# Last two expert items of a layer taken together: both down projections behind both up projections, in a two-layer trunk with routed experts

## The reference, cut to what matters

```
def hybrid_layer(x, norm1, w_in, a_ln_g, a_ln_b, a_ws, a_bs, ret_gn, w_out, norm2,
                 router_g, router_gb, router_e, router_eb, w_gate, w_up, w_down):
    bsz, seq, _ = x.shape
    h = rms_norm(x, norm1)
    z = h @ w_in
...
    x = x + jnp.concatenate([a_out, b_out, c_out], axis=-1) @ w_out
    x = x + hier_moe(rms_norm(x, norm2), router_g, router_gb, router_e, router_eb,
                     w_gate, w_up, w_down)
    return x
...
def hier_moe(h, router_g, router_gb, router_e, router_eb, w_gate, w_up, w_down):
...
    combine = jnp.sum(jax.nn.one_hot(expert_id, N_EXPERTS, dtype=jnp.float32)
                      * top_w[..., None], axis=1)
    y = jnp.zeros((n_tok, d), jnp.float32)
    for e in range(N_EXPERTS):
        he = jax.nn.silu(t @ w_gate[e]) * (t @ w_up[e])
        y = y + combine[:, e:e + 1] * (he @ w_down[e]).astype(jnp.float32)
    return y.astype(h.dtype).reshape(bsz, seq, d)
```

## Time and profile before

| | |
|---|---|
| median of 3 runs | 716.33 us (715.28 to 717.75) |
| the profiled execution | 716.53 us, of which its span is 714.6 us |
| TensorE (PE) busy | 670.8 us, 94% of the span |
| VectorE (DVE) busy | 308.9 us, 43% |
| ScalarE (ACT) busy | 191.9 us, 27% |
| read from HBM | 239.32 MB |
| granted TensorE clock | full until the last slice |

### The profile page before, as it was taken

One profiled execution on the slowest core, in us unless ns is written; L12 is line 12 of the kernel. 1 busy time (PEld: TensorE's weight loads), 2 busy tenths in 40 slices (PEclk: granted clock), 3 DMA queues, 4 the chain that ended last, 5 costly groups with the idle time before them and its releaser, 6 DMA issues.

```text
span 714.6 us, 9124 instructions
## 1 busy us (share of the span) xinstructions
PE 670.8 (94%) x3452; PEld 384.6 (54%) x3452; DVE 308.9 (43%) x605; ACT 191.9 (27%) x342; POOL 16.3 (2%) x29
## 2 busy tenths in 40 slices
PE   6998999999999999998999989999999999999984
PEld 5877778733543543542388768785353453453431
DVE  3479886711331321321474798865131331231224
ACT  3438434311201201201154445442111111111102
POOL 3000000200000000000020000000000000000000
PEclk9999999999999999999999999999999999999998
DMA  9974039999999999999986330898999999999991
GB/s 334 341 276 168 1 137 389 372 421 404 422 406 394 422 421 421 421 421 421 402 285 223 130 118 30 328 389 338 424 403 423 403 423 415 421 422 419 421 414 63
DMA packets 46026, 240.95 MB, mean 337 GB/s; under 512 B 3457, under 2 KB 3649, under 8 KB 21281
## 3 DMA queue, kind: packets, MB, share of 16 engines
q1 hardware_dynamic: 44800, 238.21, 82.8%
q0 software_dynamic: 1040, 2.04, 1.1%
q10 hardware_dynamic: 144, 0.13, 0.1%
HBM read 239.32 MB, written 1.05 MB: 336 GB/s over the span
## 4 chain that ended last, share of the span: by engine, by line
PE 74%; DMA 10%; DVE 8%; ACT 4%; issue 2%; SPq 1%; DVEq 0%; PEldq 0%; ACTq 0%
PE psum L1059 28%; PE psum L746 14%; PE psum L1091 14%; DMA up_w<-in_w_up 7%; PE psum L1043 4%; DMA down_w<-in_w_in 3%; PE psum L1004 3%; PE psum L766 2%; ACT xT L671 1%; PE psum L973 1%; DVE scores L1200 1%; PE psum L1071 1%; PE psum L914 1%; PE psum L731 1%; DVE scores L1182 1%
## 5 line engine op out<-in xcount | busy, mean ns | idle before, releaser
L746 PE MATMUL psum<-piece_hi,hT_part 128*128 128x512 f32 x416 | 130.2, 394 | 3.4 <-ACT gate_b L611 1.5
L1059 PE MATMUL psum<-up_w,xT 128*64 128x512 f32 x512 | 113.3, 594 | 4.9 <-DMA up_w<-in_w_up 4.9
L1091 PE MATMUL psum<-down_w,scores 128*64 128x512 f32 x512 | 113.5, 595 | 0.6 <-ACT scores L680 0.6
L746 PEld LDWEIGHTS psum<-piece_hi,hT_part 128*128 128x128 f32 x416 | 76.7, 188 | 21.0 <-issue 5.8
L746 PE MATMUL psum<-piece_lo,hT_part 128*128 128x512 f32 x208 | 81.2, 391 | 0.0
L1059 PEld LDWEIGHTS psum<-up_w,xT 128*64 128x64 f32 x512 | 37.7, 137 | 76.7 <-issue 68.2
L1091 PEld LDWEIGHTS psum<-down_w,scores 128*64 128x64 f32 x512 | 36.6, 137 | 64.7 <-issue 63.1
L1495 DVE TENSOR_TENSOR y_lo<-psum,y_hi 128x512 fp32r<-128x512 f32 x32 | 22.1, 691 | 110.9 <-ACT y_hi L687 110.9
L1059 PE MATMUL psum<-gate_a,xT 128*64 128x512 f32 x256 | 56.6, 593 | 1.2 <-DMA gate_a<-in_w_gate 1.2
L1059 PE MATMUL psum<-gate_b,xT 128*64 128x512 f32 x256 | 56.4, 593 | 0.0
L1474 DVE SCALAR_TENSOR_TENSOR work<-work,psum 128x512 f32<-128x512 f32 x16 | 11.0, 687 | 100.8 <-ACT work L678 100.8
(11 more groups left out here) (234 smaller groups left out, 763.2 us busy)
## 6 DMA issues: line engine op xcount, KB each, us to landing
up_w<-in_w_up SPq DMA_DIRECT2D x32, 2048.0 KB, 13.7
down_w<-in_w_down SPq DMA_DIRECT2D x64, 1024.0 KB, 11.7
gate_b<-in_w_gate SPq DMA_DIRECT2D x32, 1024.0 KB, 13.0
gate_a<-in_w_gate SPq DMA_DIRECT2D x32, 1024.0 KB, 15.9
up_w<-in_w_in SPq DMA_DIRECT2D x6, 2048.0 KB, 13.4
down_w<-in_w_in SPq DMA_DIRECT2D x4, 2048.0 KB, 21.3
down_w<-in_w_out SPq DMA_DIRECT2D x4, 2048.0 KB, 7.8
up_w<-in_w_in SPq DMA_DIRECT2D x4, 1024.0 KB, 8.4
```

The source lines that it names most:

```text
L746: ins = pe.matmul(o, src[a][:, c, t * P:(t + 1) * P], w[b][:, c, :], start=(c == 0 and n == 0), stop=(c == DC - 1 and n == len(parts) - 1))
L1059: ins = pe.matmul(psum[e * SLOTS:(e + 1) * SLOTS, bank, :], xT[:, c, k:k + SLOTS], w[:, e, c, :], start=(c == 0), stop=(c == DC - 1))
L1091: ins = pe.matmul(psum[e * SLOTS:(e + 1) * SLOTS, 2 + n, :], heT[:, c, e * SLOTS:(e + 1) * SLOTS], down_w[:, e, c, n * COLS:(n + 1) * COLS ...
```

## The change

Three edits.

**Items 6 and 7.** TensorE's `item` is cut into `gate_up` and `down`. For items 0 to 5 the two follow each other as before. For 6 and 7 the order is: gate and up of 6 (with the scatter of 5), gate and up of 7 (with no scatter), down of 6, first half of down of 7, the whole scatter of 6, second half of down of 7, scatter of 7. Since `heT` of 6 is still needed, ScalarE writes `heT` of 7 into a part of `xT` that is no longer read. ScalarE's and VectorE's steps for the sums of 6 move behind the gating of 7. SP loads gate 6, up 6, gate 7, up 7, down 6, down 7.

**Last quarter.** For items 3 and 7 the second half of down is loaded as c = 2 (two DMAs of 512 KB) and c = 3 of both experts (one DMA of 1 MiB, with a semaphore of its own, `down_quarter`), and TensorE takes both column halves of c = 2 and then both of c = 3, so that `y_summed` comes at three quarters of the half instead of at its middle.

**Table of constants.** It is issued behind CQK, the fourth piece, instead of behind BK, the second. `causal` moves into the first 256 columns, `ones` out of them; the waits for the table move to its first real users (`mask` on VectorE, `swap_score` on TensorE).

```
@@ -422,7 +430,7 @@
-                    if l == 0 and j == BK:
+                    if l == 0 and j == CQK:
                         sp.dma_start(const[:, CONST_FIRST:], table[:, CONST_FIRST:]).then_inc(const_loaded.sem, 16)
...
+                def load_down_ending(g):
+
+                    load_halves(down_w, down_d, down_loaded, downed, g, pair(g), 1, halves=(0,))
+                    sp.wait_ge(downed.sem, downed.at(g, 2 - downed.turn))
+                    settle(sp)
+                    for e in range(2):
+                        sp.dma_start(down_w[:, e, HC - 2, :], down_d[bass.ds(pair(g), 1), :, e, HC - 2, :]
+                                     .rearrange("q p n -> (q p) n")).then_inc(down_loaded[1].sem, 16)
+                    sp.dma_start(down_w[:, :, HC - 1, :], down_d[bass.ds(pair(g), 1), :, :, HC - 1, :]
+                                 .rearrange("q p e n -> (q p) e n")).then_inc(down_quarter.sem, 16)
...
-                load_down(first + 3)
-                with sp.Fori(first + 4, last, 2) as g0:
+                load_down_ending(first + 3)
+                with sp.Fori(first + 4, last, 4) as g0:
                     for o in range(2):
                         load_gate(g0 + o, o)
                         load_up(g0 + o)
                         load_down(g0 + o)
+                    for o in range(2):
+                        load_gate(g0 + 2 + o, o)
+                        load_up(g0 + 2 + o)
+                    load_down(g0 + 2)
+                    load_down_ending(g0 + 3)
...
+                    if i == PAIRS - 1:
+                        act.activation(xT[:, 0:2, 0:2 * P], psum[:, 0, :].rearrange("p (a n) -> p a n", a=2), ACT.Copy).then_inc(heT_ready.sem, 1)
+                        return
...
-                    if i > 0:
+                    if 0 < i < PAIRS - 1:
                         scatter(g0, i - 1, (0,))
                     pe.wait_ge(he_ready.sem, he_ready.item(g0, i, 1))
...
-                    for b in range(2):
+
+                def down(g0, i, parts=(0, 1)):
+
+                    for b in parts:
                         pe.wait_ge(down_loaded[b].sem, down_loaded[b].at(g0 + i, 32))
...
+                        steps = [(n, c) for n in range(2) for c in range(2 * b, 2 * b + 2)]
+                        if b == 1 and i % GROUP == GROUP - 1:
+                            steps = [(n, c) for c in range(2 * b, 2 * b + 2) for n in range(2)]
...
                     for i in range(PAIRS):
-                        item(g0, i)
+                        gate_up(g0, i)
+                        if i < PAIRS - 2:
+                            down(g0, i)
...
+                    down(g0, PAIRS - 2)
+                    down(g0, PAIRS - 1, (0,))
+                    scatter(g0, PAIRS - 2)
+                    down(g0, PAIRS - 1, (1,))
                     scatter_last(g0, PAIRS - 1)
```

More of the change, by code:

```diff
@@ L51 @@
 GELU_CUBE = 0.044715
-CONST_PARTS = [("ident", P), ("ones", P), ("logc", 3 * P), ("decay", 4 * 2 * P), ("cos", SEQ), ("sin", SEQ), ("swap", P),
-               ("before", P), ("slot", SLOTS), ("prio", EXPERTS), ("causal", P)]
+CONST_PARTS = [("ident", P), ("causal", P), ("logc", 3 * P), ("decay", 4 * 2 * P), ("cos", SEQ), ("sin", SEQ), ("swap", P),
+               ("before", P), ("slot", SLOTS), ("prio", EXPERTS), ("ones", P)]
 CONST_AT, _n = {}, 0
@@ L245, in hybrid_trunk, with heT_part @@
         heT = scores.rearrange("p j s -> p (j s)")[:, 0:HID].rearrange("p (c s) -> p c s", c=HC)
+        def heT_part(i, c, cols):
+            if i == PAIRS - 1:
+                return xT[:, c // 2, c % 2 * P + cols.start:c % 2 * P + cols.stop]
+            return heT[:, c, cols]
         mixedT = [scores.rearrange("p j s -> p (j s)")[:, 0:D].rearrange("p (c t) -> p c t", c=DC), work0.rearrange("p (c t) -> p c t", c=DC)]
@@ L306, in hybrid_trunk @@
         gate_open = signal("gate_open", 1)
+        down_quarter = signal("down_quarter", 4)
         he_ready, he_turned, heT_ready = signal("he_ready", 1), signal("he_turned", 1), signal("heT_ready", 1)
@@ L684, in item, with round_sums @@
                         copy_pick(g0, i + 1)
+                def round_sums(g0, i):
                     for n, summed_up in ((0, y_summed.item(g0, i, 1)), (1, downed.item(g0, i, 2))):
@@ L694, in _ @@
                         item(g0, i)
+                        if i < PAIRS - 2:
+                            round_sums(g0, i)
                         if i == 0:
@@ L697, in _ @@
                             act.reg_load(last, items[0:1, 1:2])
+                    for i in range(PAIRS - 2, PAIRS):
+                        round_sums(g0, i)
             last = act.value_load(items[0:1, 1:2], min_val=PAIRS, max_val=4 * PAIRS * DEPTH)
@@ L856, in _ @@
                 project(BQ)
-                pe.wait_ge(const_loaded.sem, 16)
                 pe.wait_ge(ws_loaded.sem, ws_loaded.at(l, 16))
@@ L878, in swap_score @@
                     pe.wait_ge(proj_copied_a.sem, proj_copied_a.at(l, CQK))
+                    pe.wait_ge(const_loaded.sem, 16)
                     for n in range(2):
@@ L1045, in scatter, with gate_up @@
                             ins.then_inc(scattered.sem, 1)
-                def item(g0, i):
+                def gate_up(g0, i):
                     o = i % 2
@@ L1083, in item @@
                     pe.wait_ge(heT_ready.sem, heT_ready.item(g0, i, 1))
-                    for b in range(2):
+                def down(g0, i, parts=(0, 1)):
+                    for b in parts:
                         pe.wait_ge(down_loaded[b].sem, down_loaded[b].at(g0 + i, 32))
-                        for n in range(2):
-                            if b == 0:
-                                pe.wait_ge(y_lo_ready.sem, y_lo_ready.item(g0, i, n - 1))
[L1089 to L1093, removed]
+                        steps = [(n, c) for n in range(2) for c in range(2 * b, 2 * b + 2)]
+                        if b == 1 and i % GROUP == GROUP - 1:
+                            steps = [(n, c) for c in range(2 * b, 2 * b + 2) for n in range(2)]
+                        for n, c in steps:
+                            if c == 0:
+                                pe.wait_ge(y_lo_ready.sem, y_lo_ready.item(g0, i, n - 1))
+                            if (n, c) == (0, HC - 1) and i % GROUP == GROUP - 1:
+                                pe.wait_ge(down_quarter.sem, down_quarter.at(g0, 4 * i + 4))
+                            for e in range(2):
+                                ins = pe.matmul(psum[e * SLOTS:(e + 1) * SLOTS, 2 + n, :], heT_part(i, c, slice(e * SLOTS, (e + 1) * SLOTS)),
+                                                down_w[:, e, c, n * COLS:(n + 1) * COLS], start=(c == 0), stop=(c == HC - 1))
+                            if n == 1 and c % 2 == 1:
                                 ins.then_inc(downed.sem, 1)
-                            elif b == 1:
+                            elif (n, c) == (0, HC - 1):
                                 ins.then_inc(y_summed.sem, 1)
@@ L1173, in mask @@
                     logc = C("logc")
+                    dve.wait_ge(const_loaded.sem, 16)
                     if k == 1:
@@ L1256, in _ @@
                 V.tensor_copy(qkb[:, 2:4, :], psum[:, 2:4, 0:SEQ]).then_inc(proj_copied_d.sem, 1)
-                dve.wait_ge(const_loaded.sem, 16)
                 dve.wait_ge(ws_turned.sem, ws_turned.at(l, 1))
@@ L1491, in item, with split_sums @@
                                             ALU.mult).then_inc(xT_ready_d.sem, 2 if q == 0 else 1)
+                def split_sums(g0, i):
                     for n in range(2):
@@ L1507, in _ @@
                         item(g0, i)
-                    add_items(g0, PAIRS - 1)
+                        if i < PAIRS - 2:
+                            split_sums(g0, i)
+                    for i in range(PAIRS - 2, PAIRS):
+                        split_sums(g0, i)
+                        add_items(g0, i)
                 dve.wait_ge(x_added.sem, x_added.at(last, 0))
```

## The result

| | before | after |
|---|---|---|
| median | 716.33 us (715.28 to 720.13, 5 runs) | 729.61 us (728.69 to 730.43, 5 runs) |
| ratio | | 1.0172, 95% interval 1.0142 to 1.0201 |
| span of the profiled execution | 714.6 us | 727.0 us |
| mean granted clock of it | 0.996 | 0.989 |

The change costs 13.3 us. The forecast was 6.1, in a range that ended at 726.0.

A forecast was written before the change was run, and what follows sets the result against it. TensorE and the full DMA stream were taken to bound the kernel, arriving together at item 7. Table -1.4, layer 0 +3.4, short rows +0.1, layer 1 +4.0 make +6.1 us: 722.4 us, range 718.9 to 726.0.

The forecast's parts named there:

- The wait for up 7: End of each expert half: TensorE's wait for item 7's up weights, forecast gone in layer 1 and 1.3 us in layer 0.
- its bare price: Item 7, gating to down 6 with no scatter to cover it: 2.42 us, as at item 0.
- from an empty queue: First half of down 7: the DMA queue runs empty, so 2 MiB take 7.3 us to land instead of 4.97.
- the 3.7 that the rivals name for layer 0: TensorE's standstill before down 7 in layer 0, 3.7 us as stated in the rival about a falling clock.
- the one that set the clock aside: Wait before down 7: clock assumed to stay up; its fall to 1.2 GHz was a rival, 724 to 729 us, chance 0.15.
- That row: Profile row at the program's end: granted clock still 1.00 over 4.8 us with 0.07 us of work.
- The next row: Profile entry right behind that idle stretch: clock 0.51, taken as a sign that the fall is near.
- The price given there: Clock rival's cost: down 7's halves and the scatter at half speed, 1.5 to 3.5 us per layer where it happens.
- the stream at item 3: Item 3's last-quarter loads with 4 KB rows: delay layer 0's stream, not layer 1's; 0.1 us taken.
- the table's -1.4: Prologue: table of constants issued later, ZA lands 3.1 us earlier, PE's 1.42 us wait goes; 1.4 us gained.
- The rival of a short restart: Down 7's first half lands 5.0 us after issue; each layer loses only 1.0 to 1.7 us, 717.8 us; chance 0.10.
- the fast one: End of expert halves: stream does not run empty and the quarter pays, 1.9 us earlier per layer, 711.3 us; chance 0.06.

## Why the prediction was wrong, by its own steps

**The direction and the mechanism were right.** The wait for up 7 went (0.7 and 0.8 us left in layers 1 and 0; 0 and 1.3 in the sum), gating to down 6 cost its bare price (687.59 to 690.13 is 2.5 us; 2.42 in the sum), the first half of down 7 was asked for 3.8 us after down 6 began, from an empty queue, and from the start of down 6 to its landing it took 11.4 and 11.2 us (11.1 in the sum); TensorE waited 4.2 and 4.1 us; the scatter stood on the path for 2.8 us (2.8). The last quarter was never waited for. The sum's wait is 4.1 us in layer 1; the 3.7 that the rivals name for layer 0 does not follow from it, since its own times give 4.0 (348.4 - 337.3 - 7.1).

**The step that failed is the one that set the clock aside.** I wrote that the clock was still 1.00 over 4.8 us of idleness at the program's end and gave its fall 0.15. That row shows that one idle stretch of that length passed at full clock; it does not show that such stretches do, nor that the work behind them is safe. The next row, 0.51 right behind it, said how near the fall was. In the changed kernel the clock fell inside the 4.2 us of layer 1, and in layer 0 only after a wait that had itself passed at full clock. In the 5 runs of the changed kernel the mean clock was 0.988 or 0.989, so the clock fell in each of them. The price given there, 1.5 to 3.5 us a layer, was right: 5.35 - 3.65 = 1.7 and 6.29 - 3.65 = 2.6, together 4.3, and the products in the wait gave back 4.6. The Trainium skill, TensorE: Matmul & The Clock Gate, section HAM oscillation, describes a wait for a DMA and then a burst that starts cold. The trace agrees in layer 1, where the clock was already 0.50 when the half began; in layer 0 the first microsecond behind the wait still ran at 1.00. With the clock's price in both layers the sum would have given 725 to 729.

**Mis-sized: the stream at item 3.** I took 0.1 us, for the short rows, from bounds of 0 and 0.4. In the changed kernel up 7 landed in layer 1 at 683.85, 1.3 us later than in my sum when both are set against the start of gate 7, and PE waited 0.7 us for it. The windows put the delay at item 3, but not on the rows: from 570 to 575 the stream moved 310 GB/s (419 in the kernel before), which is an estimate of 1.3 us ((421 - 310) / 421 x 5). The dip began at 570, before the DMAs of the last quarter's edit were issued (from 572.3 on), and from 575 to 585, with their last landing at 584.5, the stream ran at 410 and 428. The quarter out of the changed kernel gave 1.6 us, part of it perhaps the clock, and into the kernel before it cost 1.0, both within their intervals. About 1 us in all is likely; its cause is open.

**Not delivered: the table's -1.4.** The step itself happened in the trace; the time of the kernel with it alone leaves at most 0.3 us. My sum carried the gain through to the end because the chain behind it is PE's and VectorE's; what takes it back was not found. Single traces cannot tell: with the table alone layer 1's transposes begin at 355.36 against 358.09 before, but with the last quarter alone, and no change to the table, they begin at 355.93.

Together: 6.1 + 4.6 + 1 + 1.4 = 13.1, of 13.3 measured. The agreement is closer than the terms are known; of the three that were added only the clock's is shown by a run clear of its interval.

**The sum's other side.** The rival of a short restart fell with the landings, and the fast one with them. What the change aimed at, the waits of TensorE for up 7, was real, and a part of it could be had without the new order. At the end of an expert half two limits meet, TensorE's work behind up 7 and the stream's last transfer. Finer transfers for down alone moved nothing; finer transfers for up and down together did. That both are needed is argued from the chain, not shown, since up alone was not run.

## What to carry to other kernels

When a buffer has only one copy, ask of every new order when its last reader frees it and what is then still in the DMA queue; if nothing is, the next load costs its full latency (here 7.0 to 7.6 us for 2 MiB, 5 in a full queue) and TensorE stands still for it. Price such a standstill twice: the wait, and the half-rate clock behind it; a row that shows one idle stretch at full clock does not rule the second out, and unread matmuls in the wait take it away, if there are enough of them (16 did, 8 did not in one of two layers). Where an engine and the stream arrive together, try finer transfers on both sides first, and put movable work (here the scatter) ahead of the wait, not behind it.

## What the runs showed of the hardware that I had not expected

- Short waits seem to lower the clock too. With the scatter ahead of down 7 the waits around item 7 were at most 1 us each in the trace at hand, yet four of five runs had a mean clock of 0.990 to 0.992 and 3.5 to 6.5 us more; with nine unread products in these waits all nine runs had 0.994 or 0.995. In which wait the clock fell in those four runs, and how long their waits were, was not seen: the one trace is of the run whose clock stayed up.
- The clock can fall behind a wait, in the middle of work: in layer 0 of the changed kernel it was 1.00 through the 4.1 us of waiting and from 347 to 348, and 0.50 from 349 to 352.
- The second of two quarters from a restarted queue landed 3.4 us behind the first, where the full stream takes 2.5 for the same bytes.
- An edit that removes 1.42 us from TensorE's path in the trace need not show in the time: 12 runs leave 0.3 us.
